# First four query slabs multiplied before the norm's factor is known, and their products scaled by it

## The chip, the cores and the metric

One Trainium2 chip, one core of it. The metric is the device time of one execution in microseconds, the median of several runs. The core has five engines that run beside each other and meet only at semaphores: TensorE (PE, and PEld for its weight loads), VectorE (DVE), ScalarE (ACT), GpSimd (POOL) and SyncE (SP), which issues the loads of weights.

## What is computed

Two layers of a decoder trunk over 512 tokens with a model width of 1024. Around the change only this part of a layer matters:

```python
h = h + jnp.concatenate([o_da, o_gdn], axis=-1) @ w_out[i]
h = h + peer(rms_norm(h, ln_ffn_g[i]), peer_wq[i], peer_subkeys[i], peer_u[i], peer_v[i])

def rms_norm(x, g):
    y = xf * lax.rsqrt(jnp.mean(xf * xf, axis=-1, keepdims=True) + EPS)
    return y * g

def peer(xn, wq, subkeys, u_tab, v_tab):
    q = (xn @ wq).reshape(B, T, PEER_HEADS, 2, PEER_HALF)
    s = jnp.einsum('bthcd,hcnd->bthcn', q, subkeys)   # then top-k per head,
    ...                                               # and gelu(xn @ u) for all experts
```

The norm of a token is its residual times a weight for each of the 1024 channels (g) times one factor for the token (the reciprocal root of its mean square). The factor is the same for every channel, so (h * g * factor) @ wq equals ((h * g) @ wq) * factor.

## The kernel before

Activations lie transposed in SBUF: 128 channels on the partitions, 8 chunks (KD) of 512 tokens (T) each. `res` is the residual. Weights come as 318 slabs a layer, each 128x1024 in float32, through a ring of four buffers (RING). A slab is loaded by SP into `raw`, split by ACT into its high part `whi` (`split_hi`, L360 to L366) and by DVE into the rest, `wlo` (`split_lo`, L368 to L373), three slabs ahead of use (AHEAD). `slab_product` (L380) multiplies a slab with an activation that is split in the same way: for each of 8 chunks three matmuls (L376, L377, L378), 24 in all, into one PSUM bank. The SP queue reloads a buffer when its `wlo` is done; ACT splits into a ring slot when PE has used the slab four before.

The order within a layer is written out by hand: 28 slabs of the combined input projection, the token mixers, 8 slabs of the output projection (W_out, numbers S_OUT), then the sequence SEQ from number S_WQ on: four query slabs q0 to q3, seven slabs of the expert table U, two query slabs, seven U slabs, and so on. A query slab goes with all 512 tokens, a U slab with 384. After each second query slab PE computes `scores(hd)` (L1077, 16 matmuls on L1086), which DVE reads in `select(hd, part)` (L1468), the top-k of one head, in nine portions between the slabs that follow. The scores of head 0 come after q2 and those of head 1 after u0, in each case one slab later than the queries that they need, so that ACT can empty the bank meanwhile.

Between the last W_out slab and q0 stands the norm:

- DVE adds a W_out product to the residual (L1447), ACT squares that chunk (L686), DVE folds the eight squares into one (L414).
- PE sums the fold over the channels with eight matmuls of one column (`norm_sums`, L399), ACT takes the root (L430), DVE the reciprocal (`norm_rs`, L435), PE spreads the factor over the partitions with eight matmuls (`norm_spread`, L423) into bank 5.
- `scale_to_wide` on DVE writes `wide` = `res` times weight times factor (L450), ACT its high part `act_hi` (L460), DVE the rest `act_lo` (L443), chunk by chunk. q0 waits for `act_lo` of each chunk.
- Bank 5 is needed again by the scores of head 0, bank 4 (the sums) too. ACT copies a query product into `qt` (L714), from which the scores take their left side.

The loops over the first slabs are at L1091 (PE), L704 (ACT) and L1553 (DVE).

Of the kernel before, what the change touches and what calls it, by code (L numbers as in the profile page):

```python
# [16 lines left out]
P = 128  # L17
D = 1024
KD = D // P
T = 512  # L20
# [101 lines left out]
def trunk(nc, x_t, p_t, slabs, u_rows, w_ba, subkeys, params, consts_d, out_t):  # L122
# [4 lines left out]
    with ExitStack() as ctx:  # L127
# [105 lines left out]
        rest = place("rest", [P, 2 * NT, NKEYS], F32, m)  # L233
        topv = place("topv", [P, NT, 2, TOPK], F32, m)
# [37 lines left out]
        after_w = m[0]  # L272
        m = [late]
# [32 lines left out]
        def heads(b):  # L306
# [18 lines left out]
            mix_scaled mix_z mix_ready wout_added wq_evac subk_ready  # L325
# [54 lines left out]
        def slab_product(pe, n, slot, out, hi, lo, fresh=None, width=T):  # L380


            pe.wait_ge(s_slab_lo, n + 1)
            for k in range(KD):
                if fresh is not None:
                    pe.wait_ge(S["act_lo_ready"], fresh + k + 1)
                last = three_pass(out, whi[slot][:, k, :], wlo[slot][:, k, :], hi[:, k, 0:width], lo[:, k, 0:width],
                                  k == 0, k == KD - 1)
            last.then_inc(s_used, 1)
# [168 lines left out]
        def _(act):  # L558
            act.wait_ge(consts_loaded, 16)
            act.wait_ge(x_loaded, 16)  # L560
            with act.Fori(0, DEPTH) as layer:
# [119 lines left out]
                for k in range(KD + 1):  # L681
                    if k < KD:
                        split_hi(act, S_OUT + k + AHEAD)
                    if k > 0:
                        act.wait_ge(S["wout_added"], k)
                        nc.scalar.activation(squares[:, k - 1, :], res[:, k - 1, :], ACT.Square).then_inc(S["sq_ready"], 1)  # L686
                norm_std(act, "ffn", 1, 1.0 / D)
                act.wait_ge(s_used, S_WQ)
                act_high(act, wide, S["normed"], KD)
                act.dma_start(subk[:], subkeys[layer]).then_inc(S["subk_ready"], 16)  # L690

# [12 lines left out]
                for p in range(P_GATE):  # L704
# [3 lines left out]
                    if p == 0:  # L708
                        act.wait_ge(S["act_lo_ready"], 3 * KD)
                    if kind == "q":  # L710
                        act.wait_ge(s_used, n + 1)
                        if i >= 4:
                            act.wait_ge(S["score_ready"], i // 2 - 1)
# [159 lines left out]
        def _(pe):  # L873
            pe.wait_ge(consts_loaded, 16)
            with pe.Fori(0, DEPTH) as layer:
# [192 lines left out]
                norm_sums(pe, "ffn", 1, squares)  # L1068
                norm_spread(pe, "ffn", 1)

                def u_slab(i, k, n, slot):
# [3 lines left out]
                    slab_product(pe, n, slot, bank[2 + k % 2][:, 0:TD], act_hi, act_lo, width=TD)  # L1075

                def scores(hd):  # L1077
# [3 lines left out]
                    pe.wait_ge(S["wq_evac"], 2 * hd + 2)  # L1081
# [9 lines left out]
                for p in range(P_GATE):  # L1091
                    kind, i = SEQ[p]
                    if kind == "q":
                        if i >= 2:
                            pe.wait_ge(S["wq_evac"], i - 1)
                        slab_product(pe, S_WQ + p, p % RING, bank[i % 2][:], act_hi, act_lo, 2 * KD if p == 0 else None)
                    else:
                        u_slab(i, i % 4, S_WQ + p, p % RING)
                    if p > 0 and SEQ[p - 1][0] == "q" and SEQ[p - 1][1] % 2 == 1:
# [104 lines left out]
        def _(dve):  # L1204
# [3 lines left out]
            with dve.Fori(0, DEPTH) as layer:  # L1208
# [234 lines left out]
                act_low(dve, mixt, KD)  # L1443
                for i in range(KD):
                    split_lo(dve, S_OUT + i + AHEAD)
                    dve.wait_ge(s_used, S_OUT + i + 1)
                    V.tensor_tensor(res[:, i, :], res[:, i, :], bank[i % RING][:], ALU.add).then_inc(S["wout_added"], 1)  # L1447
                    if i >= 2:
                        fold_squares(dve, "ffn", squares, (i - 1,))
                fold_squares(dve, "ffn", squares, (KD - 1,))  # L1450
                norm_rs(dve, "ffn", 1)
                dve.wait_ge(S["wout_added"], KD)
                scale_to_wide(dve, "ffn", Q_FFN, 2 * KD)
# [99 lines left out]
                for p in range(4):  # L1553
                    split_lo(dve, S_WQ + p + AHEAD)
# [289 lines left out]
```

## Time and profile before

| what | value |
| --- | --- |
| median of three runs | 3976.68 us (3975.91 to 3977.21) |
| the profiled execution | 3971.49 us, its span 3969.7 us |
| busy in the span | PE 93%, PEld 87%, DVE 71%, ACT 37%, POOL 33% |
| mean granted TensorE clock | 0.953 of full speed |
| chain of work that ended last, by engine | PE 62%, DMA 15%, DVE 13%, issue 4% |

The profile gives, for each instruction, its start in microseconds from the start of the span and its duration. The chain of work goes back from the last instruction to whatever released each step. A matmul's record is longer than the distance to the next one, because matmuls overlap in the array: distances between starts tell what a row of matmuls costs. The granted clock is a share of 2.4 GHz; 0.5 is 1.2 GHz. Layer 1 covers about the first 1980 us, layer 2 the rest.

### The profile page before, as it was taken

Reading aid. Unit: us, or ns where it says so; the run is one execution under the profiler, and the core shown is the slowest. Engines: PE = TensorE matmul, PEld = TensorE weight load, DVE = VectorE, ACT = ScalarE, POOL = GpSimd, SP = SyncE. Lnnn points to the kernel's source line nnn. Section 1 sums busy time; section 2 is a strip of 40 time slices with the busy share of each in tenths; the row PEclk is TensorE's granted clock in tenths of the full one; section 3 lists DMA queues with packets and bytes.
Section 4 is the critical chain, followed back from the end, with each engine's and each line's share of the span. In section 5 each row is a group of like instructions: output and inputs, shape, how many; then the busy total and the mean of one; then the engine's idle time right before and its main releaser. Section 6 shows DMA issues by size and latency. Waiting matters only on the chain.

```text
span 3969.7 us, 62494 instructions
## 1 busy us (share of the span) xinstructions
PE 3677.9 (93%) x21058; PEld 3467.7 (87%) x21058; DVE 2813.0 (71%) x5900; ACT 1459.1 (37%) x2136; POOL 1290.3 (33%) x1052
## 2 busy tenths in 40 slices
PE   7987889999999999999889788899999999999997
PEld 5877779999999899899868676799999999999996
DVE  6245446889887888888562444468888878888885
ACT  4311123334675333333343111333346653333333
POOL 0000000222776446665000000002137764565650
PEclk9988879999999999999989888899999999999998
DMA  3200014445888999999222000144458899999991
GB/s 128 80 11 1 1 43 138 142 150 183 295 297 329 354 386 370 377 370 376 95 89 80 1 1 1 59 138 147 150 198 300 299 335 351 385 370 377 374 357 66
DMA packets 266280, 814.36 MB, mean 205 GB/s; under 512 B 24816, under 2 KB 106992, under 8 KB 262512
## 3 DMA queue, kind: packets, MB, share of 16 engines
q1 hardware_dynamic: 92592, 339.05, 24.1%
q0 software_dynamic: 73728, 268.47, 18.1%
q10 hardware_dynamic: 99776, 204.50, 14.4%
q8 instruction: 102, 1.67, 0.2%
q14 instruction: 82, 0.67, 0.1%
HBM read 709.16 MB, written 102.76 MB: 205 GB/s over the span
## 4 chain that ended last, share of the span: by engine, by line
PE 62%; DMA 15%; DVE 13%; issue 4%; POOL 3%; ACT 1%; DVEq 1%; ACTq 0%; SPq 0%; POOLq 0%; PEldq 0%
PE bank L376 15%; PE bank L377 15%; PE bank L378 15%; DMA gath<-slabs,rows_of 8%; DMA gath<-u_rows,rows_of 5%; PE bank L1130 4%; POOL gath L522 3%; PE bank L956 3%; PE bank L399 2%; PE bank L1049 1%; DVE wlo L373 1%; DVE acc L1689 1%; PE bank L423 1%; DVE w_lo L1655 1%; DVE act_w L1650 1%
## 5 line engine op out<-in xcount | busy, mean ns | idle before, releaser
L373 DVE TENSOR_TENSOR wlo<-raw,whi 128x1024 fp32r<-128x1024 f32 x636 | 804.2, 1265 | 442.3 <-ACT whi L366 411.6
L376 PE MATMUL bank<-act_hi,whi 128*128 128x384 f32 (+1 forms) x3008 | 1080.9, 359 | 26.2 <-DVE act_lo L443 19.4
L377 PE MATMUL bank<-act_lo,whi 128*128 128x384 f32 (+1 forms) x3008 | 1066.8, 355 | 0.0
L378 PE MATMUL bank<-act_hi,wlo 128*128 128x384 f32 (+1 forms) x3008 | 1066.3, 354 | 0.0
L366 ACT ACTIVATE whi<-raw 128x1024 fp32r<-128x1024 f32 x636 | 674.7, 1061 | 501.7 <-PE bank L378 469.7
L376 PE MATMUL bank<-w_hi,whi 128*128 128x384 f32 x2048 | 697.0, 340 | 50.5 <-DVE w_lo L1655 50.3
L514 POOL TENSOR_TENSOR onehot<-onehot,cidx 128x800 f32<-128x800 f32 x56 | 123.9, 2243 | 1814.5 <-DVEq L1538 1814.5
L378 PE MATMUL bank<-w_hi,wlo 128*128 128x384 f32 x2048 | 691.8, 338 | 0.0
L377 PE MATMUL bank<-w_lo,whi 128*128 128x384 f32 x2048 | 691.7, 338 | 0.0
L376 PEld LDWEIGHTS bank<-act_hi,whi 128*128 128x128 f32 x3008 | 570.5, 190 | 74.7 <-issue 18.8
L378 PEld LDWEIGHTS bank<-act_hi,wlo 128*128 128x128 f32 x3008 | 570.0, 189 | 39.5
L377 PEld LDWEIGHTS bank<-act_lo,whi 128*128 128x128 f32 x3008 | 570.8, 190 | 36.9
L522 POOL DMA_INDIRECT gath<-slabs,rows_of x256 | 502.9, 1965 | 279.5 <-DVE acc L1689 237.3
L522 POOL DMA_INDIRECT gath<-u_rows,rows_of x256 | 349.6, 1366 | 457.9 <-DVE gath L1623 346.5
L376 PEld LDWEIGHTS bank<-w_hi,whi 128*128 128x128 f32 x2048 | 390.4, 191 | 61.7 <-issue 61.1
L1689 DVE SCALAR_TENSOR_TENSOR acc<-gath,hi_spare,acc 128x1024 f32<-128x1024 f32 x256 | 325.5, 1283 | 101.5 <-DMA gath<-slabs,rows_of 100.7
L377 PEld LDWEIGHTS bank<-w_lo,whi 128*128 128x128 f32 x2048 | 390.4, 191 | 0.0
L378 PEld LDWEIGHTS bank<-w_hi,wlo 128*128 128x128 f32 x2048 | 389.9, 190 | 0.0
L1623 DVE SCALAR_TENSOR_TENSOR gath<-gath,lo_spare 128x1024 f32<-128x1024 f32 x256 | 309.3, 1219 | 58.0 <-DMA gath<-u_rows,rows_of 57.8
L702 ACT ACTIVATE hst<-bank 128x384 f32<-128x384 f32 x256 | 125.8, 492 | 586.0 <-PE bank L378 579.7
L791 ACT ACTIVATE w_hi<-act_w 128x384 fp32r<-128x384 f32 x256 | 133.3, 521 | 309.1 <-DVE act_w L1650 308.2
L538 POOL TENSOR_SCALAR hot<-consts,n_cols 128x128 f32<-128x128 f32 x288 | 226.2, 794 | 0.0
(287 smaller groups left out, 4065.0 us busy)
## 6 DMA issues: line engine op xcount, KB each, us to landing
raw<-slabs SPq DMA_DIRECT2D x636, 512.0 KB, 4.3
hidden_dram<-hst ACTq DMA_DIRECT2D x256, 192.0 KB, 3.3
gates_dram<-stage ACTq DMA_DIRECT2D x24, 2048.0 KB, 7.5
h_sb<-hidden_dram ACTq DMA_DIRECT2D x64, 768.0 KB, 8.5
g_sb<-gates_dram ACTq DMA_DIRECT2D x32, 1536.0 KB, 20.4
gath<-u_rows,rows_of POOLq DMA_INDIRECT x256, 8.0
gath<-slabs,rows_of POOLq DMA_INDIRECT x256, 8.6
res<-x_t SPq DMA_DIRECT2D x1, 2048.0 KB, 9.4
```

The source lines that it names most:

```text
L366: nc.scalar.activation(whi[k][:], raw[k][:], ACT.Copy).then_inc(s_slab_hi, 1)
L373: nc.vector.tensor_tensor(wlo[k][:], raw[k][:], whi[k][:].bitcast(F32), ALU.subtract).then_inc(s_slab_lo, 1)
L376: nc.tensor.matmul(out, a_hi, b_hi, start=first, stop=False)
L377: nc.tensor.matmul(out, a_hi, b_lo, start=False, stop=False)
L378: return nc.tensor.matmul(out, a_lo, b_hi, start=False, stop=last)
L522: nc.gpsimd.indirect_dma_start(gath[n % GR][:].rearrange("p k c -> p (k c)"), None, table, bass.IndirectOffsetOnAxis(ap=rows_of[:, n // P, ...
L538: last = nc.gpsimd.tensor_scalar(hot1[b % 2][:, tok, :], iota, n1_cols[b % 2][:, tok:tok + 1], None, ALU.is_equal)
L702: nc.scalar.activation(hst[k][:], bank[2 + k % 2][:, 0:TD], ACT.Gelu).then_inc(S["u_gelu"], 1)
L791: nc.scalar.activation(w_hi[r][:], act_w[r % 2][:, 0:TD], ACT.Copy).then_inc(S["w_hi_ready"], 1)
L1130: last = nc.tensor.matmul(heads(4 + i % 4)[:, s, :], hot1[b % 2][:, tok, :], hot2[b % 2][:, tok, :], start=True, stop=True)
L1623: V.scalar_tensor_tensor(gath[r][:], gath[r][:], 1.0, x_nat, ALU.mult, ALU.mult, accum_out=col).then_inc(S["gath_used"], 1)
L1689: V.scalar_tensor_tensor(acc[r % 2][:], gath[r][:], col, acc[r % 2][:], ALU.mult, ALU.add).then_inc(S["gath_used"], 1)
```

## The change

q0 to q3 no longer take `act_hi` and `act_lo` but a second pair, `q_hi` and `q_lo`, made of `res` times the weights alone, chunk by chunk in the W_out loop: ACT writes `q_hi` from `res` with the weight as a scale for each partition, DVE writes `q_lo` as (`res` times weight) minus `q_hi` in one instruction. PE runs q0, `norm_sums`, q1, `norm_spread`, q2, q3, `scores(0)`, u0, `scores(1)`. ACT copies the factor from bank 5 into `rstd_sb` in SBUF, and DVE multiplies the four query products in `qt` by it (`query_scale`). The normed activation, now in `wide_f`, with `act_hi` and `act_lo`, is made during q2, q3 and the scores, and u0 is the first to wait for it. The splits of the next slabs are written out between these steps on ACT and DVE. The scores of head 0 now come after q3. The new tiles lie in places that are free at that time.

```diff
@@ -270,6 +271,13 @@
+        h_sb_at = late
+        m = [topv_at]
+        wide_f = place("wide_f", [P, KD, T], F32, m)
+        m = [h_sb_at]
+        q_hi = place("q_hi", [P, KD, T], F32R, m)
+        q_lo = place("q_lo", [P, KD, T], F32R, m)
+        rstd_sb = place("rstd_sb", [P, T], F32, m)
@@ -377,13 +385,13 @@
             nc.tensor.matmul(out, a_hi, b_lo, start=False, stop=False)
             return nc.tensor.matmul(out, a_lo, b_hi, start=False, stop=last)
-        def slab_product(pe, n, slot, out, hi, lo, fresh=None, width=T):
+        def slab_product(pe, n, slot, out, hi, lo, fresh=None, width=T, lows="act_lo_ready"):
             pe.wait_ge(s_slab_lo, n + 1)
             for k in range(KD):
                 if fresh is not None:
-                    pe.wait_ge(S["act_lo_ready"], fresh + k + 1)
+                    pe.wait_ge(S[lows], fresh + k + 1)
                 last = three_pass(out, whi[slot][:, k, :], wlo[slot][:, k, :], hi[:, k, 0:width], lo[:, k, 0:width],
                                   k == 0, k == KD - 1)
             last.then_inc(s_used, 1)
@@ -683,11 +691,30 @@
                         split_hi(act, S_OUT + k + AHEAD)
                     if k > 0:
                         act.wait_ge(S["wout_added"], k)
+                        nc.scalar.activation(q_hi[:, k - 1, :], res[:, k - 1, :], ACT.Copy,
+                                             scale=par[:, Q_FFN + k - 1:Q_FFN + k]).then_inc(S["q_hi_ready"], 1)
                         nc.scalar.activation(squares[:, k - 1, :], res[:, k - 1, :], ACT.Square).then_inc(S["sq_ready"], 1)
+                def query(i):
+
+                    act.wait_ge(s_used, S_WQ + i + 1)
+                    nc.scalar.activation(qt[:, i, :], bank[i % 2][:], ACT.Copy).then_inc(S["wq_evac"], 1)
+
+                split_hi(act, S_WQ + AHEAD)
                 norm_std(act, "ffn", 1, 1.0 / D)
-                act.wait_ge(s_used, S_WQ)
-                act_high(act, wide, S["normed"], KD)
                 act.dma_start(subk[:], subkeys[layer]).then_inc(S["subk_ready"], 16)
+                query(0)
+                split_hi(act, S_WQ + 1 + AHEAD)
+                query(1)
+                act.wait_ge(S["rstd_bc"], bc_seen("ffn") + 1)
+                nc.scalar.activation(rstd_sb[:], bank[5][:], ACT.Copy).then_inc(S["rstd_copied"], 1)
+                split_hi(act, S_WQ + 2 + AHEAD)
+                for k in range(KD):
+                    if k == 4:
+                        query(2)
+                        split_hi(act, S_WQ + 3 + AHEAD)
+                    act.wait_ge(S["normed"], KD + k + 1)
+                    nc.scalar.activation(act_hi[:, k, :], wide_f[:, k, :], ACT.Copy).then_inc(S["act_hi_ready"], 1)
+                query(3)
                 def store_h(i, k):
@@ -701,16 +728,13 @@
                         act.wait_ge(h_stored[k], (i - k) * 4)
                     nc.scalar.activation(hst[k][:], bank[2 + k % 2][:, 0:TD], ACT.Gelu).then_inc(S["u_gelu"], 1)
-                for p in range(P_GATE):
+                for p in range(4, P_GATE):
                     kind, i = SEQ[p]
                     n = S_WQ + p
                     split_hi(act, n + AHEAD)
-                    if p == 0:
-                        act.wait_ge(S["act_lo_ready"], 3 * KD)
                     if kind == "q":
                         act.wait_ge(s_used, n + 1)
-                        if i >= 4:
-                            act.wait_ge(S["score_ready"], i // 2 - 1)
+                        act.wait_ge(S["score_ready"], i // 2 - 1)
                         nc.scalar.activation(qt[:, i % 4, :], bank[i % 2][:], ACT.Copy).then_inc(S["wq_evac"], 1)
                     else:
                         if i > 0:
@@ -1065,20 +1089,33 @@
                     if i >= RING:
                         pe.wait_ge(S["wout_added"], i - RING + 1)
                     slab_product(pe, S_OUT + i, i % RING, bank[i % RING][:], act_hi, act_lo, KD if i == 0 else None)
-                norm_sums(pe, "ffn", 1, squares)
-                norm_spread(pe, "ffn", 1)
-
-                def u_slab(i, k, n, slot):
+                for p in range(4):
+                    if p < 2:
+                        pe.wait_ge(S["wout_added"], RING + p + 1)
+                    else:
+                        pe.wait_ge(S["wq_evac"], p - 1)
+                    slab_product(pe, S_WQ + p, p, bank[p % 2][:], q_hi, q_lo, 0 if p == 0 else None,
+                                 lows="q_lo_ready")
+                    if p == 0:
+                        norm_sums(pe, "ffn", 1, squares)
+                    if p == 1:
+                        norm_spread(pe, "ffn", 1)
+
+                def u_slab(i, k, n, slot, fresh=None):
                     if not (isinstance(i, int) and i < 2):
                         pe.wait_ge(S["u_gelu"], i - 1)
-                    slab_product(pe, n, slot, bank[2 + k % 2][:, 0:TD], act_hi, act_lo, width=TD)
+                    slab_product(pe, n, slot, bank[2 + k % 2][:, 0:TD], act_hi, act_lo, fresh, width=TD)
                 def scores(hd):
                     if hd == 0:
                         pe.wait_ge(S["subk_ready"], 16)
-                    pe.wait_ge(S["wq_evac"], 2 * hd + 2)
+                    if hd < 2:
+                        pe.wait_ge(S["rstd_copied"], 1)
+                        pe.wait_ge(S["qt_scaled"], 2 * hd + 2)
+                    else:
+                        pe.wait_ge(S["wq_evac"], 2 * hd + 2)
                     if hd >= 2:
                         pe.wait_ge(S["score_read"], hd - 1)
                     for t in range(NT):
@@ -1088,15 +1125,15 @@
                                                     subk[:, 2 * hd + c, :], start=True, stop=True)
                     last.then_inc(S["score_ready"], 1)
-                for p in range(P_GATE):
+                scores(0)
+                for p in range(4, P_GATE):
                     kind, i = SEQ[p]
                     if kind == "q":
-                        if i >= 2:
-                            pe.wait_ge(S["wq_evac"], i - 1)
-                        slab_product(pe, S_WQ + p, p % RING, bank[i % 2][:], act_hi, act_lo, 2 * KD if p == 0 else None)
+                        pe.wait_ge(S["wq_evac"], i - 1)
+                        slab_product(pe, S_WQ + p, p % RING, bank[i % 2][:], act_hi, act_lo)
                     else:
-                        u_slab(i, i % 4, S_WQ + p, p % RING)
-                    if p > 0 and SEQ[p - 1][0] == "q" and SEQ[p - 1][1] % 2 == 1:
+                        u_slab(i, i % 4, S_WQ + p, p % RING, 2 * KD if p == 4 else None)
+                    if SEQ[p - 1][0] == "q" and SEQ[p - 1][1] % 2 == 1:
                         scores(SEQ[p - 1][1] // 2)
                     if p == P_XNAT:
                         pe.wait_ge(S["score_read"], PH)
@@ -1441,16 +1478,46 @@
                     if j >= H:
                         V.tensor_tensor(mixt[:, j, :], mixt[:, j, :], gzt[:, j - H, :], ALU.mult).then_inc(S["mix_ready"], 1)
                 act_low(dve, mixt, KD)
+                def query_low(k):
+
+                    dve.wait_ge(S["q_hi_ready"], k + 1)
+                    V.scalar_tensor_tensor(q_lo[:, k, :], res[:, k, :], par[:, Q_FFN + k:Q_FFN + k + 1],
+                                           q_hi[:, k, :].bitcast(F32), ALU.mult, ALU.subtract).then_inc(S["q_lo_ready"], 1)
+
                 for i in range(KD):
                     split_lo(dve, S_OUT + i + AHEAD)
                     dve.wait_ge(s_used, S_OUT + i + 1)
                     V.tensor_tensor(res[:, i, :], res[:, i, :], bank[i % RING][:], ALU.add).then_inc(S["wout_added"], 1)
+                    if i >= 1:
+                        query_low(i - 1)
                     if i >= 2:
                         fold_squares(dve, "ffn", squares, (i - 1,))
+                query_low(KD - 1)
                 fold_squares(dve, "ffn", squares, (KD - 1,))
+                split_lo(dve, S_WQ + AHEAD)
                 norm_rs(dve, "ffn", 1)
+                split_lo(dve, S_WQ + 1 + AHEAD)
+
+                def query_scale(i):
+
+                    dve.wait_ge(S["rstd_copied"], 1)
+                    dve.wait_ge(S["wq_evac"], i + 1)
+                    V.tensor_tensor(qt[:, i, :], qt[:, i, :], rstd_sb[:], ALU.mult).then_inc(S["qt_scaled"], 1)
+
+                query_scale(0)
+                query_scale(1)
                 dve.wait_ge(S["wout_added"], KD)
-                scale_to_wide(dve, "ffn", Q_FFN, 2 * KD)
+                for k in range(KD):
+                    V.scalar_tensor_tensor(wide_f[:, k, :], res[:, k, :], par[:, Q_FFN + k:Q_FFN + k + 1], rstd_sb[:],
+                                           ALU.mult, ALU.mult).then_inc(S["normed"], 1)
+                    if k == 2:
+                        split_lo(dve, S_WQ + 2 + AHEAD)
+                    if k > 0:
+                        act_low_chunk(dve, wide_f, 2 * KD, k - 1)
+                act_low_chunk(dve, wide_f, 2 * KD, KD - 1)
+                split_lo(dve, S_WQ + 3 + AHEAD)
+                query_scale(2)
+                query_scale(3)
                 tks = S["tk_chain"]
                 tk = {"n": 0}
@@ -1550,8 +1617,6 @@
                     step(V.tensor_reduce(expert[:, :, hd, :], picks, AX_X, ALU.add))
                     settle()
-                for p in range(4):
-                    split_lo(dve, S_WQ + p + AHEAD)
                 for hd in range(PH):
                     for k, parts in enumerate(((0,), (1,), (2,), (3,), (4,), (5,), (6,), (), (7,))):
                         split_lo(dve, S_WQ + 4 + HEAD_P * hd + k + AHEAD)
```

## Rows read from the trace of the kernel before

**Rows 1.** Stretches: busy us of PE, PEld, DVE, ACT, POOL; clock, DMA share, GB/s.
```profile
586.40:628.00 41.60, 35.86 (x168) 29.73 (x168) 21.40 (x41) 15.87 (x22) 0.00 (x0) 0.88 0.26 89
2558.80:2600.40 41.60, 36.12 (x169) 29.96 (x169) 21.44 (x42) 15.85 (x22) 0.00 (x0) 0.88 0.26 89
628.00:970.00 342.00, 342.00 (x1930) 330.52 (x1929) 287.36 (x1051) 112.07 (x153) 63.01 (x29) 1.00 0.46 151
```

**Rows 2.** What PE waited for, 580 to 978 us: total, times, longest.
```profile
PE bank L376 <- DVE act_lo L443: 3.0, 3, 2.4
...
PE bank L1113 <- DVEq L1598: 0.6, 1, 0.6
```

**Rows 3.** Timeline of PE, layer 1: start, us, instruction [idle before <-releaser].
```profile
586.18 0.39 PE L378 MATMUL bank<-act_hi,wlo 128*128 128x512 f32 x1
588.74 1.10 PE L399 MATMUL bank<-consts,squares 128*128 128x1 f32 x8 [2.18 <-DVE squares L414]
594.94 0.76 PE L376 MATMUL bank<-act_hi,whi 128*128 128x512 f32 x1 [2.45 <-DVE act_lo L443]
...
609.48 0.39 PE L376 MATMUL bank<-act_hi,whi 128*128 128x512 f32 x1
...
614.92 1.95 PE L1086 MATMUL bank<-subk,qt 128*128 128x128 f32 x16
...
626.35 1.95 PE L1086 MATMUL bank<-subk,qt 128*128 128x128 f32 x16
628.05 0.42 PE L376 MATMUL bank<-act_hi,whi 128*128 128x384 f32 x1
```

**Rows 4.** Timeline of PE, layer 2: last W_out matmul, first of u1.
```profile
2558.61 0.39 PE L378 MATMUL bank<-act_hi,wlo 128*128 128x512 f32 x1
...
2600.40 0.42 PE L376 MATMUL bank<-act_hi,whi 128*128 128x384 f32 x1
```

**Rows 5.** Timeline of PE: a spread between two slabs, another norm.
```profile
1329.28 1.05 PE L423 MATMUL bank<-consts,rs 128*128 128x128 f32 x8
1330.09 0.42 PE L376 MATMUL bank<-act_hi,whi 128*128 128x384 f32 x1
```

**Rows 6.** Timeline of PE: 64 one-column matmuls between two slabs, and the window of them.
```profile
148.83 10.27 PE L399 MATMUL bank<-consts,mixt 128*128 128x1 f32 x64
158.96 0.77 PE L376 MATMUL bank<-act_hi,whi 128*128 128x512 f32 x1
...
162.94 0.40 PE L376 MATMUL bank<-act_hi,whi 128*128 128x512 f32 x1
...
149.00:160.00 11.00, 11.00 (x67) 10.81 (x67) 0.00 (x0) 0.87 (x2) 0.00 (x0) 0.67 0.01 1
```

**Rows 7.** Timeline of DVE, layer 1: the norm, a split, the first top-k.
```profile
586.60 0.69 DVE L1447 TENSOR_TENSOR res<-res,bank 128x512 f32<-128x512 f32 x1 [3.01 <-PE bank L378]
587.21 1.48 DVE L414 TENSOR_TENSOR squares<-squares 128x512 f32<-128x512 f32 x2
594.71 0.74 DVE L450 SCALAR_TENSOR_TENSOR wide<-res,par,bank 128x512 f32<-128x512 f32 x1
595.37 0.69 DVE L443 TENSOR_TENSOR act_lo<-wide,act_hi 128x512 fp32r<-128x512 f32 x1
...
623.94 1.23 DVE L373 TENSOR_TENSOR wlo<-raw,whi 128x1024 fp32r<-128x1024 f32 x1 [6.02 <-ACT whi L366]
625.08 1.68 DVE L1483 MAX8 topv<-bank 128x8 f32<-128x128 f32 x8
```

**Rows 8.** Groups by line and shape: busy us, mean ns, idle before.
```profile
L450 DVE SCALAR_TENSOR_TENSOR wide<-res,par,bank 128x512 f32<-128x512 f32 x32 | 23.5, 746 | 8.8 <-PE bank L423 8.8
L1335 DVE SCALAR_TENSOR_TENSOR at_w<-at_s,at_c 128x512 f32<-128x512 f32 x8 | 6.0, 752 | 0.3
L460 ACT ACTIVATE act_hi<-wide 128x512 fp32r<-128x512 f32 x32 | 20.1, 631 | 28.7 <-DVE wide L450 28.6
L714 ACT ACTIVATE qt<-bank 128x512 f32<-128x512 f32 x32 | 19.2, 599 | 123.7 <-PE bank L378 123.7
```

More of the change, by code:

```diff
@@ L233, in trunk @@
         rest = place("rest", [P, 2 * NT, NKEYS], F32, m)
+        topv_at = m[0]
         topv = place("topv", [P, NT, 2, TOPK], F32, m)
@@ L324, in trunk @@
             rhs_ready uw_ready uw_copied step_v step_vn step_so step_state og_copied state_zero
-            mix_scaled mix_z mix_ready wout_added wq_evac subk_ready
+            mix_scaled mix_z mix_ready wout_added q_hi_ready q_lo_ready rstd_copied qt_scaled wq_evac subk_ready
             score_ready score_read tk_dve tk_act selt_ready selt_copied
```

## The prediction

> **What bounds the kernel now.** I read first the busy time by stretches [rows 1]. Behind the norm, from 628 to 970 us, PE is busy for 342.00 of 342.00 us at full clock: that stage is paced by PE, and whatever reaches it earlier ends earlier. In the 41.6 us before it, in both layers, PE is busy for only some 36 us, and its mean clock is 0.88. The waits of PE [rows 2] name `act_lo`, the last product of the norm's chain; the next slower thing in this stage is the end of the top-k, for which PE waits 0.6 us near 970. The timeline of PE [rows 3] then gives the size. The last W_out matmul starts at 586.18; with 0.227 us between matmuls (a 24-matmul slab takes 614.92 - 609.48 = 5.44 us) the next could start at 586.41. q0 starts at 594.94, and the first slab behind `scores(1)` is u1, at 628.05. So from the end of W_out to u1 there pass 41.64 us; in layer 2 it is 2600.40 - 2558.84 = 41.56 us [rows 4]. This stretch is what I recount, since its work is the same before and after, only in another order.
>
> **What PE does after the change.** Four query slabs, the sums, the spread, two score groups and u0, with no gap if nobody makes PE wait:
> - q0: 5.44. q1: 5.44 [rows 3].
> - Sums, eight one-column matmuls: 1.10 as before [rows 3], and about 0.1 for the slower first matmul behind: 1.2. They stand alone there, so this is only the nearest row.
> - Spread, eight matmuls: 1330.09 - 1329.28 = 0.81 in a stream of slabs, 0.08 more for the first matmul behind it (0.25 instead of 0.17 to the next one, as behind the scores): 0.9 [rows 5]. In this norm itself the same eight ran at half clock and took twice that, which goes away with the idle time.
> - q2, q3, scores(0), u0: the stretch from 609.48 to 626.35 holds just these four: 16.87. scores(1): 1.70 [rows 3].
>
> Sum: 5.44 + 1.2 + 5.44 + 0.9 + 16.87 + 1.70 = 31.55 us. Against 41.64 and 41.56 this is 10.1 and 10.0 us, **20.1 us in two layers**. About 8.5 of each 10 are the gap 586.41 to 594.94 less the sums and spread that remain, the rest is q0, which ran partly at half clock and on the heels of `act_lo`.
>
> **Who could make PE wait.**
> - *The low parts for q0.* The last residual chunk is added at 586.60 + 0.61. ACT then makes `q_hi` (as L460, 0.63 us [rows 8]; the scale from SBUF is not in this row, so 0.6 to 0.8), until 588.1. DVE meanwhile does `query_low(6)` and a fold, 0.66 + 0.61 from 587.21 on, then `query_low(7)`: done near 589.2. PE wants chunk 7 after 21 matmuls, at 591.2. Cover: 2 us. Chunks 0 to 5 are ready long before. If the cover went, PE would wait for the excess alone.
> - *The W_out loop.* For each 5.44 us slab DVE has a split of 1.14 (623.94 to 625.08), three steps of 0.61 or 0.66 with the new one [rows 7]: 3.1 us. ACT has a split, `q_hi` and a square, 2.3 us by rows of its like. Both stay behind PE's pace; the slab loads hang on the splits and do not move. Cost nothing.
> - *The root.* ACT waits for the sums, then DVE; they have all of q1 (5.44) for a root and a reciprocal of four columns; before, sums, root, reciprocal, spread and the first chunk together took 594.94 - 588.74 = 6.2 us [rows 3]. On ACT stand behind this wait the subkey load (its first reader, `scores(0)`, is more than two slabs away), `query(0)` and the split of slab 4. All have until q2. Nothing.
> - *Banks 0 and 1.* q2 waits for `query(0)`, which has q1's time; q3 for `query(1)`, which has q2's.
> - *The long chain behind the spread.* Call its end T0. ACT copies the factor: T0 + 0.71 (0.11 to wake, 0.60 [rows 8]). Then DVE: two scalings of queries, eight `wide_f`, eight `act_lo`, two splits, two scalings until `qt_scaled` is 4. At the distances between starts of rows 7 (0.61, 0.66, 1.14) this is 12 x 0.61 + 8 x 0.66 + 2 x 1.14 = 14.9 us, with about 0.7 for waits on ACT at the first and last chunk and 0.1 for the last one's end: T0 + 16.4. PE wants `scores(1)` at T0 - 0.2 + 16.87 = T0 + 16.7, counting the overlap of the spread's last record [rows 5]. So the cover is 0.3 us only. `wide_f` now reads SBUF only, where L450 read PSUM: such an instruction has 752 ns against 746 [rows 8], so I take the same 0.66. If it were started every 0.75 (its whole duration) the chain would be 0.7 longer and PE would wait 0.4 a layer. u0 wants its last chunk at T0 + 16.2 and gets it at T0 + 14.0: cover 2.2 us.
>
> The Trainium skill, VectorE: DVE Perf Modes, section The TRN2 errata, gives a VectorE instruction that reads SBUF 62 cycles fewer than one that reads PSUM. The trace doesn't agree (752 against 746 ns [rows 8]). By the page `wide_f` would be 65 ns cheaper, the chain 0.5 us shorter and its cover 0.8; the sum stays the same.
>
> - *DVE's later work.* `select(0, 0)` began at 625.08, 3.0 us ahead of u1; it now follows the chain and a split, T0 + 17.5, 0.9 ahead of u1. It comes 2.1 us later against PE. DVE is busy for 287 of 342 us in the stage [rows 1], so it has 55 us to take that up before the end of the top-k, on which PE waits 0.6 us. Nothing, or 0.2.
>
> ACT and DVE execute more in sum (8 `q_hi`, 8 `q_lo`, the copy, 4 scalings in a layer: some 14 us of work), all beside PE. No DMA is added.
>
> **The clock.** PE idles before the norm's matmuls and the mean clock of the stretch is 0.88; without idle time the forecast has it at 1.0 there. What speaks against: 64 one-column matmuls in a row at 148.83, with PE busy in the record 11.00 of 11 us, brought the clock to 0.67 in the window, and the next 9 matmuls took 162.94 - 158.96 = 3.98 us instead of 2.04 [rows 6]. Eight such matmuls last a tenth of that. The 16 wider ones of the scores never did it.
>
> The Trainium skill, TensorE: Matmul & The Clock Gate, section What's actually happening, says that the clock follows how busy PE has recently been. The row speaks against that in the recorded sense of busy. By the rule the change would keep the full clock for certain; by the row it is the second case below.
>
> **The rivals.**
> 1. *Forecast:* the gap goes, nothing takes its place. 20.1 us. Chance 0.78.
> 2. *The clock falls at the sums.* For: rows 6. Against: a tenth of the length. Price 1.9 us a layer; 16.3 us remain, 3960.4. Chance 0.06.
> 3. *A new wait ends last.* For: 0.3 us of cover on `scores(1)`. At 0.75 us for each three-operand step 0.4 a layer; with a microsecond more in ACT's handovers up to 1.5 a layer: 17 to 19.3 us remain, 3957 to 3960. Chance 0.09. It shows as a wait of L1086 for `qt_scaled`.
> 4. *The top-k sets the end.* DVE's late start of select is carried to 970. Price 2.1 a layer, 3960.8. Against: 55 us idle. Chance 0.02.
> 5. *Slower.* The clock stays at half from the sums until u1: a 512-token matmul takes about 0.43 instead of 0.227 (as in rows 6), so q1, q2 and q3 lose 4.8 each, u0, spread and both scores another 7.8. 22 lost against 10 won: 12 slower a layer, 4001 us. It decides from the point where some 50 of the 72 matmuls of these slabs run at half clock. Against: the clock came back after 9 matmuls even behind the 64. Chance 0.02.
> 6. *It doesn't do what it says:* q0 is still held to near its old start, by the order on DVE or ACT. Less than 8 us in sum remain. Each release for q0 is counted above with 2 us of cover, so 0.03, with what no row shows.
>
> **How the numbers follow.** The profiled execution has 3971.49 us (span 3969.7): 3971.49 - 20.1 = 3951.4 for its like. The median of the timed runs, 3976.68, is 5.2 above it; the metric is that median: 3976.68 - 20.1 = **3956.6 us**, 0.51% faster. The forecast's own range is 3954.5 to 3959, by half a microsecond a layer in the sums and in the handovers. Cases 2 to 4 end at 3961, and a small shift of unrelated waits is allowed for: **3953.5 to 3962.5**. What a measurement of this kernel can tell from no change is about 0.2%, 8 us: faster (under 3968.7) takes cases 1 to 4, 0.95; within 0.2%, case 6, 0.03; slower, case 5, 0.02.
>
> **What would show it.** In the changed kernel's profile: q0's first matmul follows W_out's last by 0.2 to 0.3 us; the distance from there to u1's first is 31.5 in both layers; granted clock 1.0 in that stretch; no row of `act_lo`, `q_lo` or `qt` among the waits of PE over 0.5 us; select(0) starts 7 to 8 us earlier than before; the stage from u1 to 970 keeps its length. Wrong would be a wait at L1086, matmuls of 0.43 us distance behind the sums, or a stage behind that has grown by what was won.

## The result and the profile after

| | before | after |
| --- | --- | --- |
| median, four runs each | 3976.3 us (3975.66 to 3977.21) | 3953.05 us (3943.91 to 3956.66) |
| ratio | | 0.9942, 95% interval 0.9927 to 0.9956 |
| profiled execution | 3971.49 us, span 3969.7 | 3956.66 us, span 3954.8 |

The kernel is 0.58% faster; 20.1 us were predicted and the medians differ by 23.2. The predicted 3956.6 us is 3.5 us above the median, which lies 0.45 us below the range (3953.5 to 3962.5). One later run of the kernel before, in a slow state at twice the usual length (7893.8 us), is left out of every figure below. The reordered stretch did what was forecast to a tenth of a microsecond; what was wrong was how still the rest of the kernel was taken to stand. Both are shown below.

The stretch from q0's first matmul to u1, in both layers, by the windows of the changed kernel (busy us and count of PE, PEld, DVE, ACT, POOL; granted clock, DMA share, GB/s), as [rows 1] before:

```profile
588.53:620.00 31.47, 31.47 (x170) 27.48 (x168) 23.34 (x38) 16.62 (x24) 0.00 (x0) 1.00 0.33 110
2551.30:2582.80 31.50, 31.50 (x169) 27.48 (x169) 23.32 (x38) 16.62 (x24) 0.00 (x0) 1.00 0.33 111
```

PE is busy throughout and the clock is 1.00, where it had been 0.88. What PE still waits for, from there to 970 us (before: [rows 2]); `act_lo` is gone, and so are the waits for the sums and the reciprocal. No new name has come: the 1.1 us for `hot` were there before with the same length:

```profile
PE bank L1167 <- POOL hot L546: 1.1, 1, 1.1
PE bank L1150 <- DVEq L1663: 0.6, 1, 0.6
```

The timeline of PE, to be laid beside [rows 3]: the last W_out matmul, the first of q0, the sums behind q0, q1, the spread, q2, both score groups, u0 and u1.

```profile
588.31 0.39 PE L386 MATMUL bank<-act_hi,wlo 128*128 128x512 f32 x1
588.53 0.40 PE L384 MATMUL bank<-q_hi,whi 128*128 128x512 f32 x1
...
594.04 0.95 PE L407 MATMUL bank<-consts,squares 128*128 128x1 f32 x8
594.85 0.48 PE L384 MATMUL bank<-q_hi,whi 128*128 128x512 f32 x1
...
600.45 1.06 PE L431 MATMUL bank<-consts,rs 128*128 128x128 f32 x8
601.26 0.47 PE L384 MATMUL bank<-q_hi,whi 128*128 128x512 f32 x1
...
612.34 1.95 PE L1123 MATMUL bank<-subk,qt 128*128 128x128 f32 x16
614.04 0.42 PE L384 MATMUL bank<-act_hi,whi 128*128 128x384 f32 x1
...
618.29 1.95 PE L1123 MATMUL bank<-subk,qt 128*128 128x128 f32 x16
619.99 0.42 PE L384 MATMUL bank<-act_hi,whi 128*128 128x384 f32 x1
```

q0 follows W_out after 0.22 us; before, the gap was 8.8 us. The whole is 619.99 - 588.53 = 31.46 us, predicted 31.55. The sums cost 594.85 - 594.04 = 0.81 us, where the prediction took 1.10. But W_out ends at 588.5 here and not at 586.4: something ahead of the change took 2.1 us more.

For that I took the starts of the same instructions in both traces and compare the lengths between them (us):

| from, to | layer 1: before, after | layer 2: before, after |
| --- | --- | --- |
| one-column sums of the q/k norm to those of the mixer norm ("mixer") | 364.00, 366.22 | 365.15, 364.10 |
| first W_out matmul to first of u1 | 86.90, 76.67 | 86.78, 76.71 |
| u1 to the last scores | 249.42, 249.42 | 249.42, 249.42 |
| last scores to the transposes near 970 | 93.46, 93.46 | 93.45, 93.46 |
| first to last gate matmul | 281.27, 281.27 | 281.29, 281.29 |
| first to last product with `w_hi` ("value stage") | 573.89, 576.06 | 570.25, 573.62 |

Only one row holds the change: 10.23 and 10.07 us less. The top-k stage repeats to 0.01 us. The mixer and the value stage, in which nothing was edited, differ, and in this pair of traces take 6.7 of the 20.3 us away (2.2 - 1.1 + 2.2 + 3.4). The spans are 14.9 us apart; the remaining 1.3 us lie in stages that the table leaves out, the largest of them 0.6.

### The profile page after: what moved, and what is told of

It is laid out like the page before. It is cut to its first block, busy times and chain, and to the rows that moved or that the text cites. A ratio compares the mean times of both kernels' runs of the same rounds, so it can differ in the third digit from the quotient of the medians.

```text
span 3954.8 us, 62544 instructions
## 1 busy us (share of the span) xinstructions
PE 3671.9 (93%) x21058; PEld 3465.5 (88%) x21058; DVE 2827.6 (71%) x5924; ACT 1469.4 (37%) x2154; POOL 1289.2 (33%) x1052
## 4 chain that ended last, share of the span: by engine, by line
PE 65%; DMA 14%; DVE 12%; issue 4%; POOL 3%; ACT 1%; DVEq 1%; SPq 0%; ACTq 0%; POOLq 0%; PEldq 0%
PE bank L384 16%; PE bank L386 16%; PE bank L385 16%; DMA gath<-slabs,rows_of 8%; DMA gath<-u_rows,rows_of 6%; PE bank L1167 4%; POOL gath L530 3%; PE bank L980 3%; PE bank L407 2%; PE bank L1073 1%; DVE acc L1754 1%; DVE wlo L381 1%; PE bank L431 1%; PE bank L1063 1%; PE bank L1062 1%
## 5 line engine op out<-in xcount | busy, mean ns | idle before, releaser
L384 PE MATMUL bank<-act_hi,whi 128*128 128x384 f32 (+1 forms) x2944 | 1053.5, 358 | 18.0 <-DVE act_lo L451 13.7
L385 PE MATMUL bank<-act_lo,whi 128*128 128x384 f32 (+1 forms) x2944 | 1040.1, 353 | 0.0
L386 PE MATMUL bank<-act_hi,wlo 128*128 128x384 f32 (+1 forms) x2944 | 1039.8, 353 | 0.0
L384 PEld LDWEIGHTS bank<-act_hi,whi 128*128 128x128 f32 x2944 | 557.6, 189 | 59.7 <-issue 13.4
L386 PEld LDWEIGHTS bank<-act_hi,wlo 128*128 128x128 f32 x2944 | 557.0, 189 | 36.5
L385 PEld LDWEIGHTS bank<-act_lo,whi 128*128 128x128 f32 x2944 | 557.9, 190 | 34.9
```

Of the source, the lines that this page charges most:

```text
L384: nc.tensor.matmul(out, a_hi, b_hi, start=first, stop=False)
L385: nc.tensor.matmul(out, a_hi, b_lo, start=False, stop=False)
L386: return nc.tensor.matmul(out, a_lo, b_hi, start=False, stop=last)
```

## Does the rest wander by itself, or did the change move it?

**The changed kernel and the kernel before once more.** No edit.

> The changed kernel once more, to see what of its time repeats. In the first trace the stretch from W_out's end to u1 took 31.46 us in layer 1 (10.2 less than before), but the value stage (first to last product with w_hi) was 2.2 and 3.4 us longer than before, and the mixer of layer 1 2.2 us longer. Theory A (the reordered stretch is fixed, mixer and value stage wander from run to run by themselves): the stretch is 31.5 again within 0.1 us, value stage and mixer lengths differ from those of the first trace by up to some 3 us in either direction, and the times spread over 5 to 15 us. Theory B (the changed order makes the later stages longer): value stages again 2 to 3 us longer than before in both layers, as in the first trace. Median of the runs by A: 3953 to 3957.

> The kernel before, once more, for a second trace of it. A: the stretch from W_out's end to u1 is 41.6 us again within 0.1; the value stages and the mixer differ from those of its first trace (573.9 and 570.3 us; 364.0 and 365.2 us) by up to 3 us. B: they repeat within 0.5 us, so that it is the changed kernel alone which wanders.

Measured, for the two kernels beside their first traces, layers 1 and 2:

| | W_out to u1 | mixer | value stage |
| --- | --- | --- | --- |
| before, first trace | 86.90, 86.78 | 364.00, 365.15 | 573.89, 570.25 |
| before, again | 86.83, 86.83 | 364.52, 366.18 | 579.55, 572.85 |
| after, first trace | 76.67, 76.71 | 366.22, 364.10 | 576.06, 573.62 |
| after, again | 76.69, 76.68 | 364.54, 364.93 | 571.23, 571.99 |

Theory A holds and B falls: the value stage of the kernel before took 5.7 us more in its second trace (more than the 3 that A allowed), and that of the changed kernel 4.8 us less. The times say the same: ten more runs of the kernel before took 3966.85 to 3980.74 us (median 3974.38), and the run of its second trace 3981.11, where its first three runs lay within 1.3 us. The changed kernel had a median of 3953.73 (3950.63 to 3967.12), ratio 0.9958 (0.9943 to 0.9974), so the medians were 20.7 us apart here.

**Smaller gathers, in both kernels.** From 970 us of a layer on, 256 indirect DMAs fetch table rows for the last 128 tokens, most of them in the value stage. There PE waits for `w_lo`, which DVE makes late because it waits for such rows. To take that away:

```diff
-                        gath[n % GR][:].rearrange("p k c -> p (k c)"), None, table,
+                        gath[n % GR][:, 0:2, :].rearrange("p k c -> p (k c)"), None, table,
```

with `table` seen as rows of a quarter's length, and four memsets for the other columns in a part of the top-k where DVE has time. Each fetch thus leaves out three quarters of its row, and it comes from another place of the table; the two differences were not parted.

> The changed kernel, with rows of 256 instead of 1024 elements fetched by the 512 gathers (from other places; the rest of each buffer is set to zero once), so the dot products and the sums of the last 128 tokens are not those of the reference. If the wandering sits in the gathers' landings: PE's waits for w_lo in the value stage shrink from 28 us to under 10, the value stage is 10 to 25 us shorter and the times spread over less than 3 us. If it doesn't: the same spread of 5 to 15 us at a time lower by the same amount.

> The kernel before with the same smaller gathers. Difference to the changed kernel with smaller gathers: by A 20.2 us (10.2 and 10.1 from the stretch) within 1 us, since nothing that wanders is left; by B 14 to 17 us, with the later stages still longer after the change.

The value stage took 533.21 us in all four layers of the two kernels: it stands still with the smaller gathers. It became 37 to 43 us shorter than in the first traces, where 10 to 25 had been expected. What DVE waited for in it, first in the kernel before, then in that with the small gathers, layer 1 (total, times, longest):

```profile
DVE acc L1689 <- DMA gath<-slabs,rows_of: 51.8, 38, 3.8
DVE gath L1623 <- DMA gath<-u_rows,rows_of: 17.0, 11, 3.4
```

```profile
DVE acc L1693 <- DMA gath<-slabs,rows_of: 11.4, 7, 2.1
DVE gath L1627 <- DMA gath<-u_rows,rows_of: 3.2, 4, 1.3
```

PE's waits for `w_lo`, 28.0 us in layer 1 of the kernel before, are gone from the view altogether. The spans of the two are 3876.1 and 3856.3 us, 19.8 apart: 10.01 and 10.19 of it from W_out to u1, 0.3 from the mixers, and -0.7 from the small stages around them. So with the value stage held still, the change is worth what its stretch shows. The medians, 3879.98 and 3858.12, lie 21.9 apart. The expectation that single runs would then spread over less than 3 us failed: they spread over 6.6 us before and over 6.4 after, but for one of 3876.08. So something else wanders too. In these two traces the only other stage that differs by more than a microsecond is the mixer, 363.9 to 365.8 us; no trace was taken of the run of 3876.08.

**The mixer.** Over the ten runs whose traces I have, with those of before and after (24 mixers), I added up from the trace's clock records how long each mixer ran at half clock (1.2 GHz). Its length goes with it, with a correlation of 0.94 and 0.35 us of length for each microsecond at half clock. The ends, and some between:

| mixer | length, us | at half clock, us |
| --- | --- | --- |
| sums times eight (below), layer 2 | 360.88 | 89.8 |
| before, layer 1 | 364.00 | 97.3 |
| after, third time (below), layer 1 | 364.58 | 100.8 |
| after, first trace, layer 1 | 366.22 | 104.0 |

The clock is thus at half for 90 to 105 us of some 364, and not for the same time in each run. Why it differs I did not try. That the clock makes the mixer longer, and doesn't only go along with longer mixers, is an inference from this relation; no experiment held it still.

**The program outside the stretch.** If the change did more than its stretch shows, the rest of the program would be shorter in the changed kernel. The span less both stretches (W_out to u1) is 3796.0, 3805.6 and 3791.3 us in the three traces with whole rows in which q0 reads `act_hi` (before, before again, and the one with matmuls of no use below), on average 3797.7. In the seven in which q0 reads `q_hi` it is 3793.1 to 3802.5, on average 3797.5. With the smaller gathers it is 3702.5 and 3702.9. So the traces show no second effect; with spreads of 7.3 and 3.5 us in so few traces, one of a few microseconds would not be seen in the first comparison.

## How much hangs on the order of the small matmuls

**Sums and spread put back ahead of q0**, which still reads `q_hi` and `q_lo`:

```diff
+                norm_sums(pe, "ffn", 1, squares)
+                norm_spread(pe, "ffn", 1)
                 for p in range(4):
...
-                    if p == 0:
-                        norm_sums(pe, "ffn", 1, squares)
-                    if p == 1:
-                        norm_spread(pe, "ffn", 1)
```

> The changed kernel with the eight sum matmuls and the spread put back ahead of q0; the query slabs still take q_hi and q_lo. It tells how much of the 10.15 us a layer (W_out's first matmul to u1: 86.9 before, 76.7 after) hangs on doing the norm's small matmuls behind slabs. Theory (idle time is what counts): PE waits for the fold, which is 1.3 us later than before because two q_lo steps stand ahead of it (590.0 against 588.7), then for the root, then spreads at half clock, 7.5 us in all where the changed kernel has 1.6; and q0 begins at half clock, some 1.5 to 2.5 us more. So 83 to 85 us from W_out to u1: only 2 to 4 of the 10.15 us remain. Rival (it is enough that q0 does not wait for act_lo): 80 us or less.

W_out to u1 took 83.86 and 83.68 us: 3.1 of the 10.15 us remain. The timeline of PE in this kernel:

```profile
588.80 1.75 PE L407 MATMUL bank<-consts,squares 128*128 128x1 f32 x8 [3.31 <-DVE squares L422]
591.11 2.08 PE L431 MATMUL bank<-consts,rs 128*128 128x128 f32 x8 [0.57 <-DVE rs L443]
592.84 0.77 PE L384 MATMUL bank<-q_hi,whi 128*128 128x512 f32 x1
594.26 0.63 PE L384 MATMUL bank<-q_hi,whi 128*128 128x512 f32 x1
...
599.80 0.39 PE L384 MATMUL bank<-q_hi,whi 128*128 128x512 f32 x1
```

The last line is the first of q1. PE now waits 3.31 us for the fold, longer than the 2.18 before [rows 3], since `query_low` stands ahead of it on DVE. The wait, the sums and the spread at half clock take 592.84 - 585.3 = 7.5 us, and q0 starts at the half clock pace (0.63 us records). With no `act_lo` to wait for it still takes 599.80 - 592.84 = 6.96 us, 1.45 more than in the changed kernel (5.51). Not waiting for `act_lo` is worth 3 us here. Putting a slab in front of each small step is worth the other 7: some 5.8 of them are the wait, the sums and the spread, the rest q0's start.

**The kernel before, with matmuls of no use in the gap.**

```diff
+                keep_busy(9)
                 norm_sums(pe, "ffn", 1, squares)
+                keep_busy(2)
                 norm_spread(pe, "ffn", 1)
+                keep_busy(9)
```

where `keep_busy(n)` issues n matmuls of 512 columns into bank 7.

> The kernel before, with matmuls of no use (512 columns, into a free bank) in the norm's gap: 9 ahead of the sums, 2 between sums and spread, 9 behind the spread. It parts the clock from the waiting: q0 ran from 594.9 to 604.2, 9.3 us for 5.44. If the clock was the cause of q0's length, W_out to u1 falls from 86.9 to 83 us. If q0 was held by the pace of act_lo (one chunk in 1.26 us), only the spread gets shorter: about 85.5 to 86, q0 still ends about 0.8 us after the last act_lo. The prediction had put this part down to both without saying which.

85.90 us in both layers, against 86.9: the second outcome. The window from just behind W_out into q1, then the first matmul of q0, one of its chunks and the first matmul of q1:

```profile
584.30:604.00 19.70, 17.47 (x75) 11.80 (x75) 14.77 (x22) 8.52 (x13) 0.00 (x0) 1.00 0.21 74
```

```profile
591.47 0.47 PE L376 MATMUL bank<-act_hi,whi 128*128 128x512 f32 x1 [0.38 <-DVE act_lo L443]
...
598.94 0.50 PE L376 MATMUL bank<-act_hi,whi 128*128 128x512 f32 x1 [0.30 <-DVE act_lo L443]
599.28 0.39 PE L377 MATMUL bank<-act_lo,whi 128*128 128x512 f32 x1
599.51 0.40 PE L378 MATMUL bank<-act_hi,wlo 128*128 128x512 f32 x1
...
600.52 0.39 PE L376 MATMUL bank<-act_hi,whi 128*128 128x512 f32 x1
```

In the kernel before q1 began here:

```profile
604.00 0.40 PE L376 MATMUL bank<-act_hi,whi 128*128 128x512 f32 x1
```

The clock is 1.00 and PE waits 0.24 to 0.38 us for `act_lo` at each of the first seven chunks. q0 takes 600.52 - 591.47 = 9.05 us, against 604.00 - 594.94 = 9.06 before with its first 5 us at a clock of 0.51. So restoring the clock alone won nothing in q0, and the 1.0 us won lies ahead of it, most of it the spread's. The two causes hide each other: with the clock full and `act_lo` in the way q0 takes 9.05 us, with `act_lo` out of the way and the clock at half at its start 6.96, with neither 5.51.

**The same filling where PE sets the pace.** In the changed kernel PE idles for 3.94 us ahead of W_out, and its next window has a clock of 0.63. Sixteen such matmuls stand there now:

```diff
                 norm_spread(pe, "mix", 2 * H)
+                for _ in range(16):
+                    nc.tensor.matmul(bank[7][:], whi[S_OUT % RING][:, 0, :], whi[S_OUT % RING][:, 2:6, :],
+                                     start=True, stop=True)
```

> The changed kernel with 16 matmuls of no use (512 columns, into a free bank) between the mixer norm's spread and the first W_out slab, where PE idles for 3.9 us and then runs 9 to 10 matmuls at half clock. In the run with such matmuls ahead of q0 the clock held, but act_lo set the pace, so it brought little; ahead of W_out the low parts come every 0.6 us, faster than three matmuls at full clock. So here the clock should be worth its price: W_out to u1 76.7 -> 74.6 to 75.2, with W_out's start at the same distance from the sums (28.3 to 28.7 us), 3 to 4 us in the two layers. If act_lo sets the pace here too, the stretch shrinks by less than 0.5 us a layer. In the times: 2 to 4 us below the changed kernel in this same call, which the spread of single runs (about 5 us each way) may hide.

> The changed kernel for the third time, beside the version with matmuls of no use and beside the kernel before on the same chip. Theory: W_out to u1 76.7 us in both layers; value stages anywhere from 570 to 577 us, mixers from 361 to 366.5 us; median 3952 to 3956, single runs from 3944 to 3967, and 20 to 22 us below the kernel before.

Windows of the first 4 us of W_out, first the changed kernel, then the filled one:

```profile
543.00:547.00 4.00, 3.67 (x10) 2.98 (x11) 4.00 (x8) 1.19 (x2) 0.00 (x0) 0.63 0.02 4
```

```profile
541.00:545.00 4.00, 3.74 (x17) 2.79 (x16) 4.00 (x8) 1.71 (x3) 0.00 (x0) 1.00 0.02 4
```

17 matmuls instead of 10 in the same time, and W_out to u1 75.10 us in both layers instead of 76.7: 1.6 us a layer, 3.2 in all, within what was expected. The times don't show it. Expected were 2 to 4 us less than the changed kernel; measured were 4.7 more, 3954.53 us (3948.74 to 3956.91) against 3949.8 (3946.69 to 3953.39) for the changed kernel beside it. In the traces its value stage in layer 1 took 574.84 us, that of the other 571.01, and this alone is more than the gain. By the stretch the filled version is the better one; by these runs that is not shown. The changed kernel repeated as expected (76.68 and 76.69; value stages 571.01 and 571.97; mixers 364.58 and 364.67), ratio to before 0.9935 (0.9922 to 0.9949). Its median was 2.2 us below the range given for it, and 25.4 us below that of the kernel before (3975.22, nine runs), where 20 to 22 had been expected.

## How near the new waits are

**The chain ahead of scores(1), made longer** by 2.35 us of DVE work of no use:

```diff
                 split_lo(dve, S_WQ + 3 + AHEAD)
+                V.tensor_tensor(winv[:].rearrange("p t h k -> p (t h k)"), res[:, 0, :], res[:, 1, :], ALU.max)
+                V.tensor_tensor(expert[:].rearrange("p t h k -> p (t h k)"), res[:, 0, :], res[:, 1, :], ALU.max)
+                V.tensor_tensor(sel[:].rearrange("p c t k -> p c (t k)"), res[:, 0:2, :], res[:, 2:4, :], ALU.max)
                 query_scale(2)
```

> The changed kernel with three DVE instructions of no use ahead of query_scale(2), 2 x 0.61 and 1.15: the chain in front of scores(1) is 2.4 us longer. In the changed kernel's trace the last scaling ends at 617.57 and PE starts scores(1) at 618.29, so 0.7 us are free (predicted: 0.3). Theory: PE waits at scores(1) for qt for 1.6 to 1.7 us a layer, W_out to u1 is 78.3 to 78.4 us instead of 76.7, and the stage behind (u1 to the last scores, 249.42 us) keeps its length: the wait comes in full and no more. Rival: there is more cover than the trace says (scores read qt late), below 77.5; or the later top-k also delays the transposes, with the stage to 970 longer than 93.45 us behind the last scores.

DVE in the changed kernel, the copied factor's first use, the first low part and the last steps of the chain:

```profile
602.17 1.29 DVE L1505 TENSOR_TENSOR qt<-qt,rstd_sb 128x512 f32<-128x512 f32 x2 [3.75 <-ACT rstd_sb L709]
603.38 1.41 DVE L1511 SCALAR_TENSOR_TENSOR wide_f<-res,par,rstd_sb 128x512 f32<-128x512 f32 x2
604.83 0.69 DVE L451 TENSOR_TENSOR act_lo<-wide_f,act_hi 128x512 fp32r<-128x512 f32 x1
...
616.29 1.28 DVE L1505 TENSOR_TENSOR qt<-qt,rstd_sb 128x512 f32<-128x512 f32 x2
617.50 1.22 DVE L381 TENSOR_TENSOR wlo<-raw,whi 128x1024 fp32r<-128x1024 f32 x1
618.63 1.68 DVE L1550 MAX8 topv<-bank 128x8 f32<-128x128 f32 x8
```

And PE at scores(1) with the longer chain:

```profile
617.82 2.02 PE L1123 MATMUL bank<-subk,qt 128*128 128x128 f32 x16 [1.61 <-DVE qt L1505]
```

PE waits 1.61 us, W_out to u1 grows by 1.87 and 1.82 us (expected 1.6 to 1.7), and the stages behind keep 249.42 and 93.45 us. The cover is therefore 2.35 - 1.85 = 0.5 us: the change lives within half a microsecond of a new wait. What goes beyond the cover comes in full, and nothing is added to it later.

**Eight times as many one-column matmuls** in this norm, in `norm_sums`:

```diff
-            for g in range(groups):
+            for g in list(range(groups)) * (8 if use == "ffn" else 1):
```

> The changed kernel with the eight one-column matmuls of this norm issued eight times over (64 instead of 8). In the changed kernel the eight cost 0.81 us between q0 and q1 and the clock stayed at 1.0. If the clock does not mind them there, the stretch grows by the time of 56 more, 5.7 to 7.3 us, to 82.4 to 84.0 us. If it falls to half as it did in the other norm of this kernel (64 in 10.1 us, and 9 slab matmuls behind at half speed), the stretch grows by 11 to 12 us, to 88, which would undo the gain: this is the mechanism that the prediction named as its second and fifth case, and it tells from how many such matmuls on it matters.

W_out to u1 took 87.79 and 87.75 us, 11.1 more than the 76.7 of the changed kernel: the whole gain and a little over. By the expectation 5.7 to 7.3 of them are the time of the 56 added matmuls at full clock, which leaves some 4 to 5 for the clock. The windows of the 64 small matmuls and of the 5 us behind them:

```profile
593.50:602.90 9.40, 9.40 (x66) 9.40 (x64) 0.00 (x0) 0.00 (x0) 0.00 (x0) 0.74 0.17 58
602.90:608.00 5.10, 5.10 (x13) 4.04 (x14) 1.40 (x2) 1.80 (x3) 0.00 (x0) 0.50 0.66 222
```

As in [rows 6] the clock falls though PE is recorded as busy for 9.40 of 9.40 us, and the slab behind starts at 0.50. So the second rival was a real mechanism; with the eight matmuls of the changed kernel (0.81 us, clock 1.00) it did not act.

## The prediction, point by point

- **The bound and the stretch.** Right: 31.46 and 31.5 us against 31.55 predicted, 10.23 and 10.07 us saved against 10.1 and 10.0. q0 is 0.22 us behind W_out, the clock 1.00. The sum of the terms was right to 0.1 us; the sums were 0.3 us cheaper than the nearest row, q slabs 0.07 dearer each.
- **q_lo's cover.** DVE ended the last `q_lo` at 591.35, 2.6 us behind the start of the last residual add at 588.73, as worked out. PE used it from 593.36 on, 2.0 us later, the predicted cover.
- **The chain behind the spread.** The cover on `scores(1)` was predicted as 0.3 us. The trace gives 618.29 - 617.57 = 0.7, the longer chain 0.5, so the wait that was feared is near but not as near as worked out. A `wide_f` step has 0.75 us and starts the next after 0.66, as taken.
- **DVE's later top-k.** It starts at 618.63, 1.4 us ahead of u1 (predicted 0.9), and the stage behind kept its length to 0.01 us: it caught up.
- **The gap and q0.** The split of each 10 us was wrong, though not its sum. The gap 586.41 to 594.94 is 8.5 us by itself; less the 2.1 for sums and spread that remain it is 6.4, and q0 has the other 3.7 (9.06 for 5.44). The step "q0 ran partly at half clock and on the heels of `act_lo`" was loose too: as long as `act_lo` set the pace, the clock cost q0 nothing.
- **The rivals.** None came true. The clock rival has been made to come true with 64 matmuls, the new wait with 2.35 us more on DVE.
- **The median and the range: wrong.** The step that failed is the last, "the metric is that median: 3976.68 - 20.1", with a range that allowed only "a small shift of unrelated waits". I took three runs within 1.3 us for the stillness of the kernel. What the runs showed in its place: over the three comparisons in which both kernels ran several times, the kernel before has a median of 3975.28 (23 runs, 3966.85 to 3980.74) and the changed one 3953.14 (15 runs, 3943.91 to 3967.12). Their means differ by 21.8 us with a standard error of 1.6, from the two spreads (3.6 and 5.4 us) and counts; 20.3 lies within that. Three more single runs of the kernel before (3971.49, 3973.61, 3981.11) change this by 0.1. In the three comparisons the medians were 23.2, 20.7 and 25.4 us apart, and the changed kernel's were 3953.05, 3953.73 and 3949.8: the second lies inside the predicted range. With such a scatter it was luck on which side of the range's end the first median fell (it missed by 0.45 us). That the range was too narrow for kernels whose single runs spread over 14 and 23 us was no luck. Of the 3.5 us by which the predicted number was off, 1.4 are the start (3976.68 against the median of the 23 runs), 0.2 the gain, and the remaining 1.9 are not told apart from the wandering of value stages (569 to 580 us) and mixers (361 to 366 us). That the change has a further effect of a microsecond or two is neither shown nor excluded by the times; the traces show no stage for it. The profiled run of before, 5.2 us below the median, was a hint in hand: one more execution of the same kernel, further away than the lower arm of the range (3.1 us).

## What to carry to other kernels

When a per-row factor commutes with a matmul, do the matmul first and put the factor's small steps behind slabs that don't need them; the gain is the idle time and what the product behind it loses by waiting chunk by chunk, and it can be counted to a tenth of a microsecond from distances between matmul starts. Less than a third of it comes from the first half of the edit alone: without `act_lo` in the way but with the small matmuls still in front, 3.1 of 10.15 us. Give the range from the parts of the kernel that wander (here waits for gathered rows and stretches at half clock), not from the spread of a few runs, and judge a change of this size by the stage and not by the total.

## What the runs showed of the hardware

- The gathers cost more than PE's waits for `w_lo` show (28.0 us in layer 1 of the kernel before): with a quarter of the bytes the value stage is 533.21 us, 40.7 less there and 35 to 46 less than in all traces with whole rows (569 to 580), and the same in each layer to 0.01 us.
- PE with one-column matmuls alone loses its clock while recorded as fully busy (0.74 over 9.4 us, then 0.50 for a slab's start); eight in a row between two slabs left it at 1.00.
- Matmuls of no use in an idle gap kept the clock at 1.00 both times. They paid (1.6 us a layer) where PE set the pace behind the gap. Where DVE did, the stretch ahead of q0 got 1.0 us shorter and q0 itself nothing (9.05 us against 9.06).
- A DVE step that reads only SBUF was not cheaper than one with a PSUM operand here: `wide_f` took 0.75 us, L450 746 ns [rows 8].
